# One state tile's matrix terms summed on GpSimd, and two output products moved on TensorE

## The chip, the cores and the metric

The kernel runs on one core of a Trainium2 chip. The metric is the device time of one launch in microseconds; lower is better. TensorE multiplies, VectorE, ScalarE and GpSimd (POOL in the profile) work on tiles, and SyncE (SP) issues the transfers. Each has its own queue and works through it in order; they meet through semaphores.

## What is computed

Two blocks of two layers on a sequence of 256 rows of width 1024, all in float32. The change lies in the last layer, whose mixer is this:

```python
def odd_mixer(h, w_in, ...):
    z = h @ w_in
    su, gc, ca, cb, gd = jnp.split(z, [...], axis=-1)
    y = s5_ssm(su, ...)
    ya, yb = jnp.split(y @ glu_w + glu_b, 2, axis=-1)
    ssm_out = ya * jax.nn.sigmoid(yb) * jax.nn.silu(gc)
    conv_out = conformer_conv(ca, cb, dw, ...) * jax.nn.silu(gd)
    return jnp.concatenate([ssm_out, conv_out], axis=-1) @ w_out
```

`s5_ssm` runs a complex linear recurrence over time, x(t) = a x(t-1) + (B u)(t), in 32 groups of 64 states, and reads it out as y = Re(C x) + d u = C_re x_re - C_im x_im + d u. `conformer_conv` is a gated causal convolution of 31 taps for each channel, a layer norm, a silu and one more product.

## The kernel before

**Weights.** A weight matrix comes in pieces of 512 rows by 512 columns (1 MB). SyncE loads a piece into a raw buffer, ScalarE rounds it to `w_hi` (L1600), VectorE subtracts to get the rest, `w_lo` (`split`, L1988), and TensorE forms each product from three: hi by hi, hi by lo, lo by hi. Both `w_hi` and `w_lo` are rings of three pieces. Three late pieces have their subtraction on GpSimd (`split`, L2851), the first half of the GLU weight among them. In the last mixer a group of 512 columns has two pieces, one for each half of the 1024 rows; `features_out` walks over the pieces i = 0, 1 and in each over four column blocks j = 0 to 3, and runs, after block (i, j), what its table `after` names. In a piece's first block the products that need `w_lo` come last (L919), after a wait for that piece's subtraction.

**The recurrence.** The 2048 states are in 16 tiles of 128, and four of these make one state tile j of the program (j = 0 to 3, 128x1024 elements for the real part and as many for the imaginary). The complex decay is turned into a real one: TensorE forms the drive (`drive(j)`, L1483), VectorE turns it by the angle -wt (`turn_back`, L2564 to L2570, which read PSUM) and scans along time with the real decay (`scan`, L2579), and GpSimd turns the result back by +wt: `turn_states(j)` forms four products with tables, x_re sin and x_im sin into `s5_o` (L2793), then x_re cos and x_im cos in place (L2796). With that

y = C_re (x_re cos) - C_re (x_im sin) - C_im (x_re sin) - C_im (x_im cos).

`outputs(j)` on TensorE (L1499) adds these four as products of 32 columns each, four column blocks apiece. The last two terms have the same matrix, and for the tiles in `SUMMED` (L112: tiles 2 and 3) they are added first, so TensorE has three products. Tile 2's sum is GpSimd's (L2801). Tile 3 has a function of its own, `turn_last_states`: GpSimd does two sine products (L2811, L2812) and one cosine product (L2814), VectorE the other (L2623) and the sum (L2631). VectorE then adds d u to the result (`outputs`, L2585) and splits y into `y_hi` and `uT_hi`.

Each tile's output comes into the same bank, `s5_o` is one buffer for all tiles, and `s5_x` is two, so `turn_states(j)` waits for `y_done` of the output before.

**The order around the change** is written out by hand. On GpSimd: tile 0, then `gate_conv` (L2784, the gate of the convolution's input), tile 1, the subtraction of a GLU piece, tile 2, tile 3, a root for the layer norm (L2688). On TensorE: column group GC with `drive(2)` after block (0, 0) and `outputs(0)` after block (0, 1); column group GD with `drive(3)` after the first piece and `outputs(1)` after block (1, 0); then the convolution as four blocks of eight tap groups (`convolve`, L1512), with `outputs(2)` ahead of block 2's last tap group; the GLU products; `outputs(3)` among them. On SyncE the 16 transfers that copy the gated input into `conv_stack` wait for `gate_conv`, and the GLU weight's two halves are loaded behind the first eight and behind all of them. On VectorE the subtractions of pieces stand between the steps of the recurrence: two after `scan(1)`, one after `turn_back(2)` (the second piece of GD) and one after `scan(3)`.

Of the kernel before, what the change touches and what calls it, by code (L numbers as in the profile page):

```python
# [44 lines left out]
HALF = 4  # L45
TAPS = 4
TAP_ROWS = 32
TAP_GROUPS = -(-CONV_K // TAPS)
# [60 lines left out]
RAW_ODD = (0, 1, 4, 0, 1, 4, 0, 1, 0, 2, 3, 1, 0)  # L109
RAW_SLOTS = [p % RAW_RING for p in range(RAW_SWITCH)] + list(RAW_ODD)  # L110
RAW_KEPT = 2
SUMMED = (2, 3)  # L112
WARM = 9
FIRST_PARTS = (((0, 1), (0,)), ((2, 3), (1, 2)), ((4, 5), (3, 4)), ((6, 7), (5, 6, 7)))
SPLIT_RING = 3
# [58 lines left out]
def build_program(nc, ins, consts, where, out):  # L174
    ctx = ExitStack()
    with ctx:
# [38 lines left out]
        def taps(a, group):  # L215
            if a < 5:
                return stack_a[:, a * channels + group, :]
            if a < 7:
                return stack_b[:, (a - 5) * channels + group, :]
            return stack_c[:, group, :]  # L220
# [650 lines left out]
        def _(pe):  # L871
# [90 lines left out]
            def features_out(n, p0, pieces, in_hi, in_lo, turn=None, after={}):  # L962


                assert turn is None
                for i in range(pieces):
                    p = p0 + i
                    pe.wait_ge(hi_ready, p + 1)
                    s = p % SPLIT_RING
                    for j in range(HALF):  # L970
                        if i == 0 and j % 2 == 0:
                            out_ready(n, j // 2)
                        at = slice(j * P, (j + 1) * P)
                        dst = OUT[j // 2][:, (j % 2) * SEQ:(j % 2 + 1) * SEQ]
                        parts = [(dst, w_hi[:, s, kk, at], w_lo[:, s, kk, at], in_hi[:, i * KP + kk, :],
                                  in_lo[:, i * KP + kk, :], True) for kk in range(KP)]
                        if j == 0:
                            last = products_upper(parts, p, i == 0, i == pieces - 1, shared=True)
                        else:
                            last = products(parts, i == 0 and j % 2 == 0, i == pieces - 1, shared=True)  # L980
                        if j == 1 and i == pieces - 1:
                            last.then_inc(out0_done, 1)
                        if j < HALF - 1 and (i, j) in after:
                            after[i, j]()
                    last.then_inc(piece_used, 1)
                    if (i, HALF - 1) in after:
                        after[i, HALF - 1]()
# [485 lines left out]
            def drive(j):  # L1473


                if j:
                    pe.wait_ge(drive_read, j)
                if j % 2 == 0:
                    pe.wait_ge(su_ready, j // 2 + 1)
                for b in range(2):  # L1480
                    for q in range(4):
                        rows_q = slice(32 * q, 32 * q + 32)
                        last = pe.matmul(bank[:, 4 + q, b * SEQ:(b + 1) * SEQ], b_mat[rows_q, b, j, :], su[rows_q, j, :],  # L1483
                                         start=True, stop=True)
                last.then_inc(drive_done, 1)

            def outputs(j):

                pe.wait_ge(states_ready, j + 1)
                if j == HALF - 1:  # L1490
                    pe.wait_ge(last_turned, 2)
                if j:
                    pe.wait_ge(y_lo, j)
                parts = [(0, s5_x[j % 2][0]), (1, s5_o[1]), (2, s5_x[j % 2][1])]
                if j not in SUMMED:
                    parts.insert(2, (2, s5_o[0]))
                for i, (m, states) in enumerate(parts):
                    for q in range(4):
                        last = pe.matmul(bank[32 * q:32 * q + 32, 2, 0:SEQ], c_mat[:, m, j, 32 * q:32 * q + 32], states[:, q, :],  # L1499
                                         start=(i == 0), stop=(i == len(parts) - 1))  # L1500
                last.then_inc(y_done, 1)

            def convolve(j, groups=range(TAP_GROUPS)):

                if j == 0 and groups[0] == 0:
                    pe.wait_ge(stack_landed, 16 * 4 * TAPS)
                    pe.wait_ge(taps_ready, 4)
                if j % 2 == 0 and groups[0] == 0:
                    pe.wait_ge(out_free[j // 2], O_USE + GD + 1)
                for a in groups:  # L1510
                    for q in range(4):
                        last = pe.matmul(OUT[j // 2][32 * q:32 * q + 32, (j % 2) * SEQ:(j % 2 + 1) * SEQ], taps(a, 4 * j + q),  # L1512
                                         conv_stack[:, j, q, TAPS * a:TAPS * a + SEQ], start=(a == 0), stop=(a == TAP_GROUPS - 1),
                                         skip_group_check=True)
                if j % 2:
                    last.then_inc(conv_done, 1)

            def block_out(p, blocks, banks, in_hi, in_lo, first, rows_ready):
# [12 lines left out]
                if blocks[-1] == KP - 1:  # L1531
# [3 lines left out]
                         after={(0, 0): turn_su, (0, 2): lambda: drive(0)})  # L1535
            features_out(O_USE + CB, O_PIECE + 2 * CB, 2, hT_hi, hT_lo,
                         after={(0, 0): lambda: drive(1)})
            features_out(O_USE + GC, O_PIECE + 2 * GC, 2, hT_hi, hT_lo,
                         after={(0, 0): lambda: drive(2), (0, 1): lambda: outputs(0)})
            features_out(O_USE + GD, O_PIECE + 2 * GD, 2, hT_hi, hT_lo,  # L1540
                         after={(0, HALF - 1): lambda: drive(3), (1, 0): lambda: outputs(1)})
            convolve(0)
            convolve(1)
            convolve(2, range(0, TAP_GROUPS - 1))
            outputs(2)
            convolve(2, range(TAP_GROUPS - 1, TAP_GROUPS))
            convolve(3)

            def y_rows(kk):
                pe.wait_ge(y_lo, kk + 1)  # L1550
# [1133 lines left out]
        def _(pool):  # L2684
# [101 lines left out]
            def turn_states(j):  # L2786
# [8 lines left out]
                for i, v in enumerate(s5_x[j % 2]):  # L2795
                    last = pool.tensor_tensor(v, v, cos, ALU.mult)  # L2796
                    if i == 0 or j in SUMMED:
                        order.mark(last)
                if j in SUMMED:
                    order.settle()  # L2800
# [125 lines left out]
```

## Time and profile before

| | |
|---|---|
| median of 3 runs | 992.45 us (992.42 to 992.67) |
| the profiled execution, its own time | 992.89 us |
| its span | 991.1 us |
| TensorE busy, share of the span | 984.2 us, 99% |
| VectorE busy | 732.6 us, 74% |
| ScalarE busy | 497.3 us, 50% |
| GpSimd busy | 129.8 us, 13% |

The profile is of one execution. Its span runs from the first instruction to the last, and the time of the execution is 1.8 us longer. A busy share is an average over the whole kernel: GpSimd's 13% lies mostly in the last 130 us, where it is the state tiles' engine and busy nearly without pause, and that is where the change is.

### The profile page before, as it was taken

The numbers are of one execution on the slowest core, as the hardware profiler recorded it, in microseconds if no ns is written. First come the engines' busy times: TensorE is split into PE (matmuls) and PEld (weight loads), VectorE is DVE, ScalarE is ACT, GpSimd is POOL, SyncE is SP. The second block draws the span as 40 slices with busy tenths as digits, with TensorE's granted clock in tenths as the row PEclk, the third lists the DMA queues.
The fourth block names the chain that finished last, engine by engine and source line by source line (L and its number), as shares of the span: only waits on it lengthen the run. The fifth ranks groups of instructions, "written<-read, shape, count | busy, mean of one in ns | idle before, by whom it ended". The sixth has DMA issues, their size and how long they took to land.

```text
span 991.1 us, 13299 instructions
## 1 busy us (share of the span) xinstructions
PE 984.2 (99%) x5502; PEld 835.6 (84%) x5502; DVE 732.6 (74%) x836; ACT 497.3 (50%) x596; POOL 129.8 (13%) x101
## 2 busy tenths in 40 slices
PE   9999999999999999999999999999999999999997
PEld 8888888888888888888888888888887899899796
DVE  5867786776656656677786777888877777789984
ACT  6545553554444345444563454444478554644252
POOL 0000000000000000000000030000000159169720
PEclk9999999999999999999999999999999999999999
DMA  9897796546655564697796667555554965345451
GB/s 362 300 280 266 234 281 209 197 168 212 197 185 170 185 216 132 192 300 247 234 273 219 222 176 243 200 184 207 170 173 153 300 193 173 126 170 155 112 191 43
DMA packets 116764, 204.33 MB, mean 206 GB/s; under 512 B 10209, under 2 KB 29665, under 8 KB 116449
## 3 DMA queue, kind: packets, MB, share of 16 engines
q1 hardware_dynamic: 116704, 203.50, 62.8%
q8 instruction: 43, 0.70, 0.3%
q14 instruction: 17, 0.13, 0.0%
HBM read 189.09 MB, written 12.06 MB: 203 GB/s over the span
## 4 chain that ended last, share of the span: by engine, by line
PE 99%; DVE 0%; ACT 0%; DVEq 0%; issue 0%; ACTq 0%
PE bank L887 13%; PE bank L889 13%; PE bank L890 13%; PE bank L1219 12%; PE bank L910 10%; PE bank L914 9%; PE bank L921 9%; PE bank L1223 6%; PE bank L1301 2%; PE bank L1512 1%; PE bank L1001 1%; PE bank L1091 1%; PE bank L919 1%; PE bank L912 1%; PE bank L1499 1%; PE bank L1173 1%
## 5 line engine op out<-in xcount | busy, mean ns | idle before, releaser
L1988 DVE TENSOR_TENSOR w_lo<-arena,w_hi 128x2048 fp32r<-128x2048 f32 (+1 forms) x79 | 181.5, 2309 | 80.5 <-ACT w_hi L1600 80.1
L1988 DVE TENSOR_TENSOR w_lo<-raw,w_hi 128x2048 fp32r<-128x2048 f32 (+1 forms) x78 | 178.1, 2293 | 70.3 <-ACT w_hi L1600 69.9
L1600 ACT ACTIVATE w_hi<-raw 128x2048 fp32r<-128x2048 f32 (+1 forms) x83 | 157.0, 1892 | 93.2 <-PE bank L890 63.8
L1600 ACT ACTIVATE w_hi<-arena 128x2048 fp32r<-128x2048 f32 (+1 forms) x79 | 149.4, 1891 | 97.7 <-PE bank L890 72.7
L1219 PE MATMUL bank<-hT,w_hi 128*128 128x512 f32 x504 | 123.4, 391 | 0.0
L1219 PEld LDWEIGHTS bank<-hT,w_hi 128*128 128x128 f32 x504 | 92.2, 188 | 17.6
L887 PE MATMUL bank<-w_hi,hT 128*128 128x512 f32 (+1 forms) x240 | 91.9, 383 | 0.0
L2688 POOL TENSOR_TENSOR rstd<-mean,const 128x1 f32<-128x1 f32 (+1 forms) x16 | 9.1, 578 | 628.0 <-DVE mean L1997 458.9
L889 PE MATMUL bank<-w_lo,hT 128*128 128x512 f32 (+1 forms) x224 | 85.5, 381 | 0.0
L890 PE MATMUL bank<-w_hi,hT 128*128 128x512 f32 (+1 forms) x224 | 85.5, 381 | 0.0
L887 PE MATMUL bank<-w_hi,uT_hi 128*128 128x512 f32 x208 | 81.1, 390 | 0.0
L890 PE MATMUL bank<-w_hi,uT_lo 128*128 128x512 f32 x208 | 80.9, 389 | 0.0
L889 PE MATMUL bank<-w_lo,uT_hi 128*128 128x512 f32 x208 | 80.9, 389 | 0.0
L910 PE MATMUL bank<-w_hi,hT 128*128 128x512 f32 (+1 forms) x208 | 79.8, 386 | 0.0
L914 PE MATMUL bank<-w_hi,hT 128*128 128x512 f32 (+1 forms) x208 | 78.9, 382 | 0.0
L1223 PEld LDWEIGHTS bank<-hT,w_lo 128*128 128x128 f32 x504 | 67.1, 191 | 3.9
L910 PE MATMUL bank<-w_hi,uT_hi 128*128 128x512 f32 x176 | 68.9, 392 | 0.0
L914 PE MATMUL bank<-w_hi,uT_lo 128*128 128x512 f32 x176 | 68.7, 390 | 0.0
L1223 PE MATMUL bank<-hT,w_lo 128*128 128x256 f32 x504 | 68.3, 282 | 0.0
L887 PE MATMUL bank<-hT,w_hi 128*128 128x256 f32 x192 | 55.3, 289 | 0.0
L921 PE MATMUL bank<-w_lo,hT 128*128 128x512 f32 (+1 forms) x208 | 53.9, 381 | 0.0
L887 PEld LDWEIGHTS bank<-w_hi,hT 128*128 128x128 f32 x240 | 45.1, 188 | 8.7
(339 smaller groups left out, 1854.4 us busy)
## 6 DMA issues: line engine op xcount, KB each, us to landing
arena<-in_w_in SPq DMA_DIRECT2D x21, 1024.0 KB, 5.3
raw<-in_w_in SPq DMA_DIRECT2D x20, 1024.0 KB, 7.0
arena<-in_w_up SPq DMA_DIRECT2D x16, 1024.0 KB, 5.7
raw<-in_w_up SPq DMA_DIRECT2D x16, 1024.0 KB, 5.8
arena<-in_w_down SPq DMA_DIRECT2D x16, 1024.0 KB, 5.1
raw<-in_w_down SPq DMA_DIRECT2D x16, 1024.0 KB, 5.1
raw<-in_e_w_in SPq DMA_DIRECT2D x6, 1024.0 KB, 5.5
arena<-in_e_w_in SPq DMA_DIRECT2D x6, 1024.0 KB, 5.3
```

Source lines behind the costliest of these rows:

```text
L887: pe.matmul(dst, a_hi, b_hi, start=first, stop=False, skip_group_check=shared)
L889: pe.matmul(dst, a_hi, b_lo, start=False, stop=False, skip_group_check=shared)
L890: mm = pe.matmul(dst, a_lo, b_hi, start=False, stop=last_one, skip_group_check=shared)
L910: pe.matmul(dst, a_hi, b_hi, start=(start and i == 0), stop=False, skip_group_check=shared)
L912: pe.matmul(dst, a_hi, b_lo, start=False, stop=False, skip_group_check=shared)
L914: pe.matmul(dst, a_lo, b_hi, start=False, stop=False, skip_group_check=shared)
L921: mm = pe.matmul(dst, a_hi, b_lo, start=False, stop=last_one, skip_group_check=shared)
L1219: pe.matmul(UP[j], w_hi[:, s[i], kk, at[j]], hT[:, k, :, :].rearrange("p e t -> p (e t)"), start=(i == kk == 0), stop=False, skip_group_ch ...
L1223: return pe.matmul(UP[j][:, 0:SEQ], w_lo[:, s[i], kk, at[j]], hT_hi[:, i * KP + kk, :], start=False, stop=(i == 1 and kk == KP - 1), skip_ ...
L1301: last = pe.matmul(OUT[t], a[:, KP * i + k, at[t]], w[:, s[i], k, :], start=(first and k == 0), stop=(last_one and k == KP - 1))
L1600: act.activation(w_hi[:, p % SPLIT_RING, :, 0:n], raw_at(p)[:, :, 0:n], copy).then_inc(hi_ready, 1)
L1988: dve.tensor_tensor(w_lo[:, s, :, 0:n], raw_at(p)[:, :, 0:n], w_hi[:, s, :, 0:n].bitcast(F32), ALU.subtract).then_inc(lo_ready, 1)
```

## The change

`SUMMED` gets tile 0. GpSimd then adds x_im cos and x_re sin of tile 0 after the four products, and `outputs(0)` has three products for four. `outputs(0)` moves from block (0, 1) of GC's first piece to behind its block (0, 3). `outputs(2)` moves behind the last tap group of convolution block 2 and the first two of block 3. The condition at `conv_done` keeps the count of that semaphore as it was, now that block 3 comes in two calls.

```diff
-SUMMED = (2, 3)
+SUMMED = (0, 2, 3)
...
-                if j % 2:
+                if j % 2 and groups[-1] == TAP_GROUPS - 1:
                     last.then_inc(conv_done, 1)
...
             features_out(O_USE + GC, O_PIECE + 2 * GC, 2, hT_hi, hT_lo,
-                         after={(0, 0): lambda: drive(2), (0, 1): lambda: outputs(0)})
+                         after={(0, 0): lambda: drive(2), (0, HALF - 1): lambda: outputs(0)})
...
             convolve(2, range(0, TAP_GROUPS - 1))
+            convolve(2, range(TAP_GROUPS - 1, TAP_GROUPS))
+            convolve(3, range(0, 2))
             outputs(2)
-            convolve(2, range(TAP_GROUPS - 1, TAP_GROUPS))
-            convolve(3)
+            convolve(3, range(2, TAP_GROUPS))
```

GpSimd's queue from tile 0 to tile 1, before: two sine products, two cosine products, `gate_conv`, and the first instructions of tile 1.

```order
L2793 TENSOR_TENSOR h_sb<-arena 128x1024 [waits scans_done]
L2793 TENSOR_TENSOR h_sb<-arena 128x1024
L2796 TENSOR_TENSOR arena<-arena 128x1024 [waits pool_order]
L2796 TENSOR_TENSOR arena<-arena 128x1024
L2784 TENSOR_TENSOR arena<-arena 128x4x256 [waits out_free1,out_free0]
L2793 TENSOR_TENSOR h_sb<-arena 128x1024 [waits y_done,scans_done]
```

The same place after the change (every line number here is one higher):

```order
L2794 TENSOR_TENSOR h_sb<-arena 128x1024 [waits scans_done]
L2794 TENSOR_TENSOR h_sb<-arena 128x1024
L2797 TENSOR_TENSOR arena<-arena 128x1024 [waits pool_order]
L2797 TENSOR_TENSOR arena<-arena 128x1024
L2802 TENSOR_TENSOR arena<-arena,h_sb 128x1024 [waits pool_order]
L2785 TENSOR_TENSOR arena<-arena 128x4x256 [waits out_free1,out_free0]
L2794 TENSOR_TENSOR h_sb<-arena 128x1024 [waits y_done,scans_done]
```

The add is new and waits for the products (`pool_order`); `gate_conv` and all of tile 1 stand one instruction later.

TensorE's queue at the third output, in the convolution (`const`, `stack_b` and `stack_c` hold the taps of groups 0 to 4, 5 and 6, and 7, four matmuls a group; L1499 is `outputs(2)`):

```order
 L1512 MATMUL bank<-arena,stack_b 32x256 x8
+L1512 MATMUL bank<-arena,stack_c 32x256 x4
+L1512 MATMUL bank<-arena,const 32x256 x8
 L1499 MATMUL bank<-arena,c_mat 32x256 [waits y_lo,states_ready]
 L1499 MATMUL bank<-arena,c_mat 32x256 x3
 L1499 MATMUL bank<-h_sb,c_mat 32x256 x4
 L1499 MATMUL bank<-arena,c_mat 32x256 x4
-L1512 MATMUL bank<-arena,stack_c 32x256 x4
-L1512 MATMUL bank<-arena,const 32x256 x20
+L1512 MATMUL bank<-arena,const 32x256 x12
```

Twelve matmuls (three tap groups) now stand ahead of the third output that stood behind it. In the trace each of these matmuls is two records.

## Rows read from the trace of the kernel before

**Rows 1.** The chain of waits over the whole span, shares by engine
```profile
PE 99%; DVE 0%; ACT 0%; DVEq 0%; issue 0%; ACTq 0%
```

**Rows 2.** Timeline of TensorE, first output (start us, us, engine, line, instructions)
```profile
901.72 0.64 PE L1499 MATMUL bank<-arena,c_mat 128*32 128x256 f32 x8
902.17 1.05 PE L1499 MATMUL bank<-h_sb,c_mat 128*32 128x256 f32 x16
903.03 0.61 PE L1499 MATMUL bank<-arena,c_mat 128*32 128x256 f32 x8
903.58 0.39 PE L887 MATMUL bank<-hT,w_hi 128*128 128x256 f32 x1
...
906.56 0.28 PE L910 MATMUL bank<-hT,w_hi 128*128 128x256 f32 x1
```

**Rows 3.** Timeline of TensorE around the second output
```profile
920.30 0.64 PE L919 MATMUL bank<-hT,w_lo 128*128 128x256 f32 x4
...
920.87 0.64 PE L1499 MATMUL bank<-arena,c_mat 128*32 128x256 f32 x8
```

**Rows 4.** Timeline of TensorE, first rows of the third and last outputs
```profile
937.20 0.61 PE L1499 MATMUL bank<-arena,c_mat 128*32 128x256 f32 x8
...
949.30 0.64 PE L1499 MATMUL bank<-arena,c_mat 128*32 128x256 f32 x8
```

**Rows 5.** Timeline of GpSimd, 896 to 948 us (x2: two instructions)
```profile
896.39 4.76 POOL L2796 TENSOR_TENSOR arena<-arena 128x1024 f32<-128x1024 f32 x2
...
901.09 2.21 POOL L2784 TENSOR_TENSOR arena<-arena 128x1024 f32<-128x1024 f32 x1
...
912.40 4.78 POOL L2796 TENSOR_TENSOR arena<-arena 128x1024 f32<-128x1024 f32 x2
...
919.82 4.60 POOL L2851 TENSOR_TENSOR w_lo<-raw,w_hi 128x2048 fp32r<-128x2048 f32 x1 [2.64 <-DVE w_lo L1988]
...
924.82 4.77 POOL L2793 TENSOR_TENSOR h_sb<-arena 128x1024 f32<-128x1024 f32 x2 [0.40 <-DVE arena L2579]
...
934.49 2.39 POOL L2801 TENSOR_TENSOR arena<-arena,h_sb 128x1024 f32<-128x1024 f32 x1
...
938.85 2.79 POOL L2811 TENSOR_TENSOR h_sb<-arena 128x1024 f32<-128x1024 f32 x1 [1.98 <-PE bank L1499]
...
941.60 2.39 POOL L2812 TENSOR_TENSOR h_sb<-arena 128x1024 f32<-128x1024 f32 x1
...
944.07 3.26 POOL L2814 TENSOR_TENSOR arena<-arena 128x1024 f32<-128x1024 f32 x1
```

**Rows 6.** Timeline of GpSimd, the two sine products of tile 1, each by itself
```profile
903.83 4.07 POOL L2793 TENSOR_TENSOR h_sb<-arena 128x1024 f32<-128x1024 f32 x1 [0.53 <-PE bank L1499]
907.86 4.46 POOL L2793 TENSOR_TENSOR h_sb<-arena 128x1024 f32<-128x1024 f32 x1
```

**Rows 7.** Timeline of VectorE, two weight splits in a row, each by itself
```profile
903.37 2.26 DVE L1988 TENSOR_TENSOR w_lo<-raw,w_hi 128x2048 fp32r<-128x2048 f32 x1
905.55 4.49 DVE L1988 TENSOR_TENSOR w_lo<-raw,w_hi 128x2048 fp32r<-128x2048 f32 x1
```

**Rows 8.** Timeline of VectorE, single rows from 898 to 949 us
```profile
898.70 4.75 DVE L2579 TENSOR_TENSOR_SCAN arena<-bank,arena 128x256 f32<-128x256 f32 x8
...
917.45 2.29 DVE L1988 TENSOR_TENSOR w_lo<-arena,w_hi 128x2048 fp32r<-128x2048 f32 x1
...
937.13 2.27 DVE L1988 TENSOR_TENSOR w_lo<-raw,w_hi 128x2048 fp32r<-128x2048 f32 x1
...
941.68 3.39 DVE L2623 TENSOR_TENSOR arena<-arena 128x1024 f32<-128x1024 f32 x1 [1.01 <-POOL h_sb L2811]
...
947.27 1.21 DVE L2631 TENSOR_TENSOR arena<-arena,h_sb 128x1024 f32<-128x1024 f32 x1
```

**Rows 9.** Timeline of ScalarE, split of the first half of the GLU weight
```profile
915.96 1.92 ACT L1600 ACTIVATE w_hi<-raw 128x2048 fp32r<-128x2048 f32 x1 [2.56 <-DMA raw<-in_o_glu_w]
```

**Rows 10.** Timeline of SyncE's queue, load of that half
```profile
908.68 1.26 SPq L703 DMA_DIRECT2D raw<-in_o_glu_w  x1
```

## The prediction, written before the changed kernel ran

> **What bounds the kernel now.** I read the chain of waits first: it is TensorE for 99% of the span [rows 1]. So time is won only by giving TensorE less to do, and lost wherever it has to wait. The timeline of TensorE, from 901 us to the end, shows no idle row: at each of the four output products the gap ahead is about 0.1 us beyond the usual spacing, after weights of another shape, and not a wait. Then I read the timelines of the engines that feed it, to see how close to TensorE's need each of them delivers.
>
> Two deliveries are close. The lower half of the second weight piece of group GD, a VectorE subtraction at 917.45, ends at 917.45 + 2.29 = 919.74 [rows 8]; TensorE starts the four products that read it at 920.30 [rows 3]. And VectorE's sum for the last output ends at 947.27 + 1.21 = 948.48 [rows 8]; that output starts at 949.30 [rows 4]. The slack is 0.56 and 0.82 us.
>
> The third thing to see is that GpSimd and VectorE do not run side by side when VectorE reads both inputs from SBUF. GpSimd's sine product of a 128x1024 tile takes 2.39 us alone [rows 5], but 4.07 and 4.46 us while VectorE splits weights [rows 6]; in that stretch the second of two splits takes 4.49 us where the first took 2.26 [rows 7]. The starts interleave: split 1 until 905.6, product 1 until 907.9, split 2 until 910.0, product 2 until 912.3. Each waits for the other's instruction to end, and the one that waits goes next. Scans and operations on PSUM do not do this: two cosine products took 4.76 us beside VectorE's scan [rows 5, 8]. The Trainium skill ("SBUF — State Buffer", Who interferes with whom) says just this: a VectorE instruction with two SBUF inputs and a GpSimd one that reads SBUF exclude each other for the whole instruction, and issue order decides who is blocked. It is the rule that speaks against this change, and the trace agrees.
>
> **The change, part by part.**
>
> *One product fewer.* In the first output 16 matmul records on h_sb take 903.03 - 902.17 = 0.86 us [rows 2], so the eight of one term take 0.43. TensorE gains **0.43 us**.
>
> *The first output stands later.* It moves behind the other half of the group's first piece, which ran from 903.58 to 906.56 [rows 2], some 2.9 us without the switch of weights; so it starts at 901.7 + 2.9, about 904.6. It needs GpSimd's new add. The cosine products end at 896.39 + 4.76 = 901.15; with the 0.08 us that such a settle costs and 2.39 us for an add [rows 5] the states are ready at **903.6**. No wait: 1 us of slack. The move itself costs nothing.
>
> *The add on GpSimd.* 2.39 us, beside a scan on VectorE, so the price is not there but behind it. In the queue behind it stand gate_conv (2.21 us, before at 901.09 [rows 5]) and the four products of the second tile. I replay the exclusion with the measured times:
> - split 1 is issued at 903.37 and waits for the add, which lets go at about 903.5; the next VectorE instruction starts at 905.7.
> - gate_conv, which ran free before, now waits for split 1: it ends at 907.9. Split 2 then: VectorE is free at 909.95, as before, when split 2 ended at 905.55 + 4.49 = 910.04 [rows 7].
> - VectorE's chain is thus unmoved: its third split is issued at about 917.45 again.
> - GpSimd's first sine product ends at 912.3, where before the *second* ended. The four products end 2.3 us later than the 917.18 of before (912.40 + 4.78 [rows 5]), at 919.5, and the last cosine product starts at 917.1, **0.3 us ahead of the split**. So the split waits until 919.4 and ends at 919.4 + 2.26 = **921.7**.
>
> TensorE reaches the products that read it at 920.30 - 0.43 = 919.87. A wait's release, a weight load and the first matmul take another 0.1, so they start at about 921.8: TensorE stands **1.5 us later** than before (921.8 - 920.3), the saving already in it. The wait is 1.9 us. The second output needs states at 920.87 before; they are ready at 919.5, so it waits for nothing more.
>
> *SyncE, ScalarE.* gate_conv releases the 16 transfers of the convolution stack and, between them, half a GLU weight. gate_conv ends 4.6 us later, so that load's issue moves from 908.68 [rows 10] to 913.3 and ScalarE's split of it from 915.96 [rows 9] to 920.5; it ends at 922.45. GpSimd's own split of that piece (919.82 before [rows 5]) starts then, 2.6 us later, and the third tile's first product at 927.1, not 924.82. The third states were ready at 934.49 + 2.39 = 936.88; now about 939.2.
>
> *The third output stands later.* Three column groups of the convolution pass ahead of it; the one that it already skips and two more, 8 records each, at 0.43: 1.3 us. TensorE comes to it at 937.20 + 1.5 + 1.3 = 940.0 [rows 4]. That is past 939.2, so the move covers GpSimd's delay; at its old place TensorE would have waited some 0.5 us. But the last tile's GpSimd work waits for this output's end. It started at 938.85 [rows 5], now 938.85 + 2.8 = 941.65. Before, it was held for 0.4 us (2.79 against 2.39) by the split at 937.13 [rows 8]; that split, 1.9 late too, is over at 941.3. First sine 944.05, second 946.4 (before 941.60 + 2.39 = 943.99), so 2.4 later. VectorE's cosine product, which before ran 3.39 us for the same exclusion [rows 8], the third GpSimd product and VectorE's sum keep their distances: the sum ends at 948.48 + 2.4 = 950.9. TensorE gets to the last output at 949.30 + 1.5 = 950.8 and starts at about 951.0. That is another 0.15.
>
> *After that* only the rows of TensorE count; ScalarE and VectorE follow it with the same shift.
>
> **Sum.** -0.43 + 1.93 (wait for the split) + 0.15 (last output) = **+1.65 us**. The profiled execution took 992.89, 0.44 over the median of 992.45; against the median that is **994.1**. If nothing were blocked, the sum would be -0.43 and the result 992.0; 0.43 is also all the change can win.
>
> Bounds of the unknown: the order at 903.5 and at 917, and how fast the GLU load lands once it starts later, between the 7.3 us of before (908.68 to 915.96) and about 8.5.
>
> **The rivals.**
> 1. *GpSimd goes first at 903.5* (gate_conv ahead of split 1). For: its instruction is already in its queue when the add ends. Against: at 905.6 and 907.9 the engine that waited went next. Then both splits run later, VectorE is 2.35 us late at 912.3, its third split is no longer blocked but ends at 922.05; TensorE stands 1.9 later there, 2.05 at the end: 994.5.
> 2. *The third split gets in ahead of the last cosine product* (margin 0.3 us). Then TensorE has its weights, but the states of the second tile come at 922.0 against 920.87 - 0.43: 1.2 later, and 1.45 after the last output: 993.9.
> 3. *The load lands late.* Each us past 0.8 us of slack on the third states goes to TensorE, and to the last tile's chain behind it: 994.6 to 995.2.
> 4. *Not slower.* GpSimd's queue has room after all: if the add and gate_conv pass while VectorE scans and its splits do not meet them, cosine products end by 919.4 with the split done in time (it has 0.13 us of slack left against 919.87). It decides at one blocked instruction less, 2.2 us, between 903 and 917. Price -0.43 to +0.1: 992.0 to 992.6. Against: between 901.15 and 919.87 stand one add, gate_conv, four products and three splits, 2.39 + 2.2 + 9.6 + 6.6 = 20.8 us, in 18.7 us, and they exclude each other.
>
> **How the numbers follow.** Forecast 0.57; rival 1, 0.12; rival 2, 0.10; rival 3, 0.12; rival 4, 0.07; 0.02 for anything else. Forecast and rivals 1 and 2 share a cause and lie at 993.9 to 994.5; each carries some 0.5 us for what I read off the starts of rows. The range 993.3 to 995.0 leaves out rival 4 and the far end of rival 3, some 0.13. What a measurement can tell from no change is about 0.2%, 1.98 us, so the border is 994.43, just above my forecast. Faster by that much is out of reach of 0.43: 0.01. Within it lie most of the forecast's own spread (0.6 us), rivals 2 and 4: 0.63. Slower: rivals 1 and 3 and a part of the forecast, 0.36.
>
> **What would show it.** In the new profile: an idle row of TensorE, about 1.9 us, ahead of the L919 products near 921.8, released by VectorE's split; that split 4.2 us long; gate_conv longer than 4 us, ending near 907.9; GpSimd's second-tile products ending near 919.5; the first transfer of the stack near 908; a short wait at the last output. I am wrong if L919 starts before 920.5, or if the first or third output has a wait ahead of it.

## The result, and the profile after

The changed kernel takes 994.45 us in the median of 13 executions, the kernel before 992.45 in as many; the ratio is 1.0021 with a 95% interval of 1.0013 to 1.0029. Measured a second time, 11 executions: 994.19 us, 1.0019 (1.0010 to 1.0028). So the change makes the kernel slower by 1.6 to 2.0 us (the second time the kernel before, run beside it, had a median of 992.56). That is small, but both intervals lie above 1: it is a loss and not noise. One of the first 13 executions took 1999.65 us, with 128x512 matmuls of 674 ns where they take 391 otherwise, and it is the one that was profiled; so what follows is the profile of an execution of the second measurement, 994.33 us long with a span of 992.5.

| | before | after |
|---|---|---|
| median | 992.45 us | 994.45 us, again 994.19 |
| profiled execution, its span | 992.89, 991.1 us | 994.33, 992.5 us |
| executions of the first measurement, lowest to highest (without the one of 1999.65) | 992.35 to 992.79 | 993.86 to 996.02 |

The last row is news: the changed kernel is spread over 2.2 us. The kernel before stays within 0.5 us here, and within 1.0 us (992.23 to 993.26) in all its 104 executions beside the kernels below.

TensorE's waits in the last 190 us, for which the kernel before has no row at all (columns: engine, tile, line, released by: us in total, times, longest):

```profile
PE bank L919 <- DVE w_lo L1989: 1.6, 1, 1.6
```

TensorE's timeline of the same kernel, at its four outputs and the products of the late weight piece:

```profile
904.44 0.64 PE L1499 MATMUL bank<-arena,c_mat 128*32 128x256 f32 x8
904.89 0.61 PE L1499 MATMUL bank<-h_sb,c_mat 128*32 128x256 f32 x8
905.32 0.61 PE L1499 MATMUL bank<-arena,c_mat 128*32 128x256 f32 x8
905.87 0.39 PE L910 MATMUL bank<-hT,w_hi 128*128 128x256 f32 x1
...
921.47 0.74 PE L919 MATMUL bank<-hT,w_lo 128*128 128x256 f32 x4 [1.60 <-DVE w_lo L1989]
...
922.14 0.64 PE L1499 MATMUL bank<-arena,c_mat 128*32 128x256 f32 x8
...
939.74 0.61 PE L1499 MATMUL bank<-arena,c_mat 128*32 128x256 f32 x8
...
950.72 0.64 PE L1499 MATMUL bank<-arena,c_mat 128*32 128x256 f32 x8
```

The first output now takes 905.87 - 904.44 = 1.43 us where it took 903.58 - 901.72 = 1.86 [rows 2]: the 0.43 us are won. Then TensorE stands idle ahead of L919, which starts at 921.47 and not at 920.30 [rows 3]. From there to the last output it takes 950.72 - 921.47 = 29.25 us, 0.25 more than before [rows 3, 4]. Together the last output starts 950.72 - 949.30 = 1.42 us later, and that is the whole difference of the two profiled executions (994.33 - 992.89 = 1.44 us).

GpSimd's timeline of the changed kernel (x2: two instructions in one row):

```profile
901.06 2.40 POOL L2802 TENSOR_TENSOR arena<-arena,h_sb 128x1024 f32<-128x1024 f32 x1
903.42 4.25 POOL L2785 TENSOR_TENSOR arena<-arena 128x1024 f32<-128x1024 f32 x1
907.63 6.83 POOL L2794 TENSOR_TENSOR h_sb<-arena 128x1024 f32<-128x1024 f32 x2
914.53 4.74 POOL L2797 TENSOR_TENSOR arena<-arena 128x1024 f32<-128x1024 f32 x2
922.13 4.59 POOL L2852 TENSOR_TENSOR w_lo<-raw,w_hi 128x2048 fp32r<-128x2048 f32 x1 [2.87 <-ACT w_hi L1601]
926.68 4.77 POOL L2794 TENSOR_TENSOR h_sb<-arena 128x1024 f32<-128x1024 f32 x2
...
936.37 2.38 POOL L2802 TENSOR_TENSOR arena<-arena,h_sb 128x1024 f32<-128x1024 f32 x1
941.40 2.39 POOL L2812 TENSOR_TENSOR h_sb<-arena 128x1024 f32<-128x1024 f32 x1 [2.65 <-PE bank L1499]
```

VectorE's timeline, the splits and the sum for the last output:

```profile
903.22 6.60 DVE L1989 TENSOR_TENSOR w_lo<-raw,w_hi 128x2048 fp32r<-128x2048 f32 x2
...
917.22 4.19 DVE L1989 TENSOR_TENSOR w_lo<-arena,w_hi 128x2048 fp32r<-128x2048 f32 x1
...
938.81 2.27 DVE L1989 TENSOR_TENSOR w_lo<-raw,w_hi 128x2048 fp32r<-128x2048 f32 x1
...
949.41 1.21 DVE L2632 TENSOR_TENSOR arena<-arena,h_sb 128x1024 f32<-128x1024 f32 x1
```

Read the three together. The add takes 2.40 us beside a scan. `gate_conv`, 2.21 us before [rows 5], takes 4.25, because the first split is in its way. The pair of splits takes 6.60, as before. The two cosine products run from 914.53 to 919.27, and the third split, issued at 917.22 while the second of them runs, takes 4.19 us for 2.29 [rows 8]. It ends at 921.41, and TensorE goes on 0.06 later.

One thing said of GpSimd ahead of the prediction was too strong. It is not busy nearly without pause over the last 130 us: there it is busy 69.3 of 131 us. Around the change it nearly is, 50.0 of the 57 us from 893 to 950.

### The profile page after: what moved, and what is told of

It is laid out like the page before. It is cut to its first block, busy times and chain, and to the rows that moved or that the text cites. A ratio compares the mean times of both kernels' runs of the same rounds, so it can differ in the third digit from the quotient of the medians.

```text
span 1997.8 us, 13284 instructions
## 1 busy us (share of the span) xinstructions
PE 1991.1 (100%) x5494; PEld 1392.2 (70%) x5494; DVE 738.8 (37%) x836; ACT 502.0 (25%) x596; POOL 117.2 (6%) x102
## 4 chain that ended last, share of the span: by engine, by line
PE 100%; DVE 0%; ACT 0%; DVEq 0%; issue 0%; ACTq 0%
PE bank L887 13%; PE bank L890 13%; PE bank L889 13%; PE bank L1219 12%; PE bank L910 10%; PE bank L921 9%; PE bank L914 9%; PE bank L1223 6%; PE bank L1301 2%; PE bank L1512 1%; PE bank L1001 1%; PE bank L1091 1%; PE bank L912 1%; PE bank L919 1%; PE bank L1499 1%; PE bank L1173 1%
## 5 line engine op out<-in xcount | busy, mean ns | idle before, releaser
L1219 PE MATMUL bank<-hT,w_hi 128*128 128x512 f32 x504 | 245.8, 674 | 0.0
L1219 PEld LDWEIGHTS bank<-hT,w_hi 128*128 128x128 f32 x504 | 149.0, 304 | 70.3 <-issue 63.3
L887 PE MATMUL bank<-w_hi,hT 128*128 128x512 f32 (+1 forms) x240 | 159.0, 663 | 0.0
L889 PE MATMUL bank<-w_lo,hT 128*128 128x512 f32 (+1 forms) x224 | 147.5, 659 | 0.0
L890 PE MATMUL bank<-w_hi,hT 128*128 128x512 f32 (+1 forms) x224 | 145.7, 650 | 0.0
L887 PE MATMUL bank<-w_hi,uT_hi 128*128 128x512 f32 x208 | 140.8, 677 | 0.0
L889 PE MATMUL bank<-w_lo,uT_hi 128*128 128x512 f32 x208 | 139.7, 671 | 0.0
L890 PE MATMUL bank<-w_hi,uT_lo 128*128 128x512 f32 x208 | 139.6, 671 | 0.0
L1223 PEld LDWEIGHTS bank<-hT,w_lo 128*128 128x128 f32 x504 | 125.8, 324 | 17.8 <-issue 16.6
L910 PE MATMUL bank<-w_hi,hT 128*128 128x512 f32 (+1 forms) x208 | 138.0, 664 | 0.0
L914 PE MATMUL bank<-w_hi,hT 128*128 128x512 f32 (+1 forms) x208 | 136.9, 659 | 0.0
L1223 PE MATMUL bank<-hT,w_lo 128*128 128x256 f32 x504 | 128.2, 440 | 0.0
L914 PE MATMUL bank<-w_hi,uT_lo 128*128 128x512 f32 x176 | 119.1, 677 | 0.0
L910 PE MATMUL bank<-w_hi,uT_hi 128*128 128x512 f32 x176 | 119.0, 676 | 0.0
L921 PE MATMUL bank<-w_lo,hT 128*128 128x512 f32 (+1 forms) x208 | 104.6, 655 | 0.0
L889 PEld LDWEIGHTS bank<-w_lo,hT 128*128 128x128 f32 x224 | 70.2, 314 | 34.3 <-issue 31.6
L921 PE MATMUL bank<-w_lo,uT_hi 128*128 128x512 f32 x176 | 91.3, 674 | 0.0
```

The source lines that it names most:

```text
L887: pe.matmul(dst, a_hi, b_hi, start=first, stop=False, skip_group_check=shared)
L889: pe.matmul(dst, a_hi, b_lo, start=False, stop=False, skip_group_check=shared)
L890: mm = pe.matmul(dst, a_lo, b_hi, start=False, stop=last_one, skip_group_check=shared)
L910: pe.matmul(dst, a_hi, b_hi, start=(start and i == 0), stop=False, skip_group_check=shared)
L914: pe.matmul(dst, a_lo, b_hi, start=False, stop=False, skip_group_check=shared)
L921: mm = pe.matmul(dst, a_hi, b_lo, start=False, stop=last_one, skip_group_check=shared)
```

## The experiments

Apart from the repetition, each kernel takes one or two causes away or puts one in another place. `small_add`, `small_gate`, `small_cosine` and `cosine_load` leave out a part of the arithmetic and `four_products` counts a term twice: their times tell what a piece of work costs, and none of them is a kernel to use. Each was timed beside the kernel before, whose medians in three groups were 992.56 (the first four), 992.43 (the next four) and 992.48 (the last four). "Exclusion theory" in the expectations is the prediction's account: GpSimd and VectorE hold each other up, and VectorE's third split comes late.

### The changed kernel again

> The changed kernel once more, for a profile of an execution at full TensorE clock. Exclusion theory: 994.1 to 994.5; the third split on VectorE (L1989, near 917.4) lasts about 4.2 us because the last cosine product of tile 1 holds it up, gate_conv (L2785) lasts over 4 us, and TensorE waits about 1.9 us ahead of the L919 products near 921.8. Rival, the moved outputs: no wait there, but waits at the third or the last output that sum to 2 us.

994.19 us. The rows above are its profile: the wait, the long split and the long `gate_conv` are there.

### The moves without the sum

```diff
-SUMMED = (0, 2, 3)
+SUMMED = (2, 3)
```

> SUMMED is (2, 3) again, both outputs stay where the change puts them. Exclusion theory: the moves alone cost the 1.3 us by which the third output's end is late, less 0.8 us of slack at the last output and 0.4 us that GpSimd's first product of tile 3 no longer waits: 992.5 to 992.9. If the moves are the cause, nearly the whole loss stays: 994.3 or more.

992.69 us (992.42 to 992.99), ratio 1.0000 (0.9992 to 1.0009). The moves cost next to nothing, as foreseen. They are cleared, and the loss needs the sum. VectorE's third split is already held here, 4.26 us long, and does no harm: it ends at 918.97, and TensorE is there at 919.76. Its row on VectorE:

```profile
914.71 4.26 DVE L1989 TENSOR_TENSOR w_lo<-arena,w_hi 128x2048 fp32r<-128x2048 f32 x1
```

### The sum on a sixteenth of the time steps

```diff
-                    last = pool.tensor_tensor(s5_x[j % 2][1], s5_x[j % 2][1], s5_o[0], ALU.add)
+                    part = slice(0, 16 if j == 0 else SEQ)
+                    last = pool.tensor_tensor(s5_x[j % 2][1][:, :, part], s5_x[j % 2][1][:, :, part], s5_o[0][:, :, part], ALU.add)
```

> The change with GpSimd's add of tile 0 on 16 of 256 time steps (the other steps of that sum are left out, so that matrix term is incomplete); TensorE still has three products. Exclusion theory: the add's 2.2 us are what pushes the rest of GpSimd's queue back; without them gate_conv and tile 1 stand where they stood, the third split lasts 2.3 us, and the 0.43 us of the product is a gain: 992.0 to 992.4. If the moves are the cause: 994 or more.

992.38 us (992.19 to 992.66). TensorE has all of the change's relief and order here, and the loss is gone: without the add's 2 us on GpSimd there is none. But not all of the story in the expectation is right. GpSimd's and VectorE's timelines of this kernel (first GpSimd):

```profile
901.13 2.20 POOL L2785 TENSOR_TENSOR arena<-arena 128x1024 f32<-128x1024 f32 x1
905.90 6.44 POOL L2794 TENSOR_TENSOR h_sb<-arena 128x1024 f32<-128x1024 f32 x2 [2.57 <-PE bank L1499]
912.42 4.77 POOL L2797 TENSOR_TENSOR arena<-arena 128x1024 f32<-128x1024 f32 x2
```

```profile
903.00 4.69 DVE L1989 TENSOR_TENSOR w_lo<-raw,w_hi 128x2048 fp32r<-128x2048 f32 x2
...
915.09 4.25 DVE L1989 TENSOR_TENSOR w_lo<-arena,w_hi 128x2048 fp32r<-128x2048 f32 x1
```

The third split is held here as well, 4.25 us. GpSimd stands idle until 905.90 for the first output's end, so the two splits of the pair run nearly undisturbed, 4.69 us for 6.60, and VectorE comes to its third split 2.1 us sooner, again behind a cosine product that has begun. I had expected the split to be short. What decides is not whether it is held but when the product ahead of it ends: here at 917.19, in the changed kernel at 919.27, and each time the split ends 2.1 us behind it, at 919.34 and 921.41. TensorE wants its result at 919.49 here.

### The gate on a sixteenth of the time steps

```diff
-                pool.tensor_tensor(c_at, c_at, gate_d[:, :, :], ALU.mult).then_inc(conv_gated, 1)
+                pool.tensor_tensor(c_at[:, :, 0:16], c_at[:, :, 0:16], gate_d[:, :, 0:16], ALU.mult).then_inc(conv_gated, 1)
```

> The change in full, but gate_conv multiplies 16 of 256 time steps (the gate of the convolution's input is left out on the rest). Exclusion theory: GpSimd has 2 us less to do between the add and the second tile, so the last cosine product ends near 917.7 and the third split near 919.9, when TensorE needs it: 992.1 to 992.8. If the add's own delay of the first output were the cause, this would change nothing: 994.3.

992.27 us (992.04 to 992.76). The add is whole here, and the loss is gone again. It is not the add as such: 2 us less at another place in GpSimd's queue do the same. The last cosine product ends at 917.46 and the third split, held for 4.22 us, at 919.61, in time for TensorE at 919.74. Two things go together in this kernel, since `gate_conv` also ends 1.8 us sooner than in the changed one and releases its transfers sooner.

### Four products again, beside the sum

```diff
-                if j not in SUMMED:
+                if j not in SUMMED or j == 0:
```

> The change, but TensorE forms the first output of four products again (the sine term is then counted twice in tile 0; nothing else differs). Exclusion theory: TensorE stands idle until VectorE's third split anyway, so the 0.43 us of the product only shortens that wait: 994.0 to 994.4, the same as the change, and the wait ahead of L919 is 1.2 us for 1.6. If the saved product is a gain that the rest merely outweighs: 994.6.

994.64 us in the median (993.89 to 996.18): outside the range that I gave, and the rival's figure. But the executions are spread over 2.3 us, and the lowest are 993.89 and 993.92, where the changed kernel's lowest are 993.86 and 994.01: the product made no difference to the shortest executions. The profile is of its slowest execution. TensorE's timeline there:

```profile
921.79 0.74 PE L919 MATMUL bank<-hT,w_lo 128*128 128x256 f32 x4 [1.22 <-DVE w_lo L1989]
...
941.30 0.64 PE L1499 MATMUL bank<-arena,c_mat 128*32 128x256 f32 x8 [1.04 <-POOL arena L2802]
```

The wait at L919 is 1.22 us, 0.38 shorter, as the exclusion theory has it: the saved product only lengthens a wait. And there is a second wait, at the third output. ScalarE's timeline of this execution, and then of the changed kernel, shows where it starts:

```profile
922.58 1.91 ACT L1601 ACTIVATE w_hi<-raw 128x2048 fp32r<-128x2048 f32 x1 [9.08 <-DMA raw<-in_o_glu_w]
```

```profile
920.08 1.91 ACT L1601 ACTIVATE w_hi<-raw 128x2048 fp32r<-128x2048 f32 x1 [7.28 <-DMA raw<-in_o_glu_w]
```

The half GLU weight, whose load now stands behind a later `gate_conv`, landed 2.5 us later in the one than in the other. GpSimd's split of it, its tile 2 and with them the third states came later by as much. A later issue is not needed for that: in `small_add` the same load is issued at 908.69, as in the kernel before (908.68 [rows 10]), and ScalarE gets it at 919.04 and not at 915.96 [rows 9].

### The last cosine product of tile 1 on a sixteenth

```diff
-                    last = pool.tensor_tensor(v, v, cos, ALU.mult)
+                    part = slice(0, 16 if i == 1 and j == 1 else SEQ)
+                    last = pool.tensor_tensor(v[:, :, part], v[:, :, part], cos[:, :, part], ALU.mult)
```

> The change, but GpSimd's last cosine product of tile 1 covers 16 of 256 time steps (the turn of that part is left out on the rest). Add and gate_conv stay. Exclusion theory: the third split is no longer held, lasts 2.3 us and ends near 919.6, TensorE does not wait ahead of L919: 992.1 to 992.7. If the later gate_conv with its transfers is the cause (it ends at 907.7 here too): 994.

993.62 us (993.29 to 994.31): between the two figures, and a miss. The split does last 2.29 us, and no wait is left ahead of L919. TensorE's timeline shows what is left:

```profile
919.75 0.64 PE L919 MATMUL bank<-hT,w_lo 128*128 128x256 f32 x4
...
939.42 0.64 PE L1499 MATMUL bank<-arena,c_mat 128*32 128x256 f32 x8 [1.30 <-POOL arena L2803]
```

I had counted only one of the two things that the late GpSimd queue moves. The other, `gate_conv` and the load behind it, ends in a wait of 1.3 us at the third output (this profile is of the slowest execution, 994.31 us, so in the median one the wait is probably shorter). In the changed kernel that wait is hidden by the first one: its third states are ready at 938.75, and TensorE comes at 939.74 only because it stood idle ahead of L919. They are two causes side by side, and the later one counts.

### The second half's load earlier

```diff
                 if s == 1:
                     load(square_piece(ins["o_glu_w_2"][0], 0, 0))
-            load(square_piece(ins["o_glu_w_2"][0], 1, 0))
+                if s == 2:
+                    load(square_piece(ins["o_glu_w_2"][0], 1, 0))
```

> The change, with the load of the GLU weight's second half put ahead of the last four stack transfers. In the profile of the changed kernel ScalarE waited for that load until 929.7, between two steps that free TensorE's banks and split y. Exclusion theory: the median stays, 994.0 to 994.3, since the wait ahead of L919 does not depend on it; the load explains the executions above 994.6 if it explains anything, and they should be gone. If late transfers are the main cause: 993.0 or less.

995.82 us in 5 executions (995.37 to 996.17): worse than the change, and a second miss. TensorE's waits in this kernel's last 190 us:

```profile
PE bank L1513 <- DMA arena<-arena: 1.8, 1, 1.8
PE bank L920 <- DVE w_lo L1990: 1.6, 1, 1.6
```

The megabyte went ahead of the last four stack transfers (of the sixteen into `conv_stack`), and the convolution (L1513) waited 1.8 us for them. So the stack, whose first transfer is issued 4.4 us later than before, is a third thing that the late `gate_conv` brings near the edge: its last transfer lands 5.9 us ahead of the convolution in the kernel before (921.33 and 927.24), 2.6 us ahead in the changed kernel and 0.5 us ahead in `small_cosine`.

### GpSimd waits for the split

```diff
+                    if i == 1 and j == 1:
+                        piece_split(pool, O_PIECE + 2 * GD + 1)
                     last = pool.tensor_tensor(v, v, cos, ALU.mult)
...
-                         after={(0, HALF - 1): lambda: drive(3), (1, 0): lambda: outputs(1)})
+                         after={(0, HALF - 1): lambda: drive(3), (1, 1): lambda: outputs(1)})
```

> The change, with GpSimd's last cosine product of tile 1 made to wait for VectorE's third split, and the second output one block later on TensorE, where its states are ready. Exclusion theory: the split lasts 2.3 us and TensorE does not wait ahead of L919, but the cosine product ends 2.2 us later and the third and last outputs wait in turn, 1.1 and 0.2 us: 993.2 to 993.8. If the split's hold is not the cause: 994.2 or more.

993.76 us (993.21 to 994.46). The split is 2.29 us again, L919 does not wait, and the rest has moved to the second, third and last output (0.27, 0.95 and 0.37 us in its profile).

### The first half's load ahead of everything

```diff
+            load(square_piece(ins["o_glu_w_2"][0], 0, 0))
             sp.wait_ge(conv_gated, 1)
             piece_split(sp, RAW_SWITCH - 1)
...
-                if s == 1:
-                    load(square_piece(ins["o_glu_w_2"][0], 0, 0))
```

This edit was laid on the change, on `small_cosine` and on `split_first`.

> The change, with the load of the GLU weight's first half ahead of the stack transfers and of their wait for gate_conv. Two-cause theory (the held split sets the floor, the load, late behind gate_conv, sets the spread above it): the floor stays, the spread goes: median 993.8 to 994.2, highest 994.5 or less. If the spread has nothing to do with this load, it stays up to 996.

994.28 us (993.99 to 996.25). The floor (the shortest executions) stays. The spread stays too: 4 of 10 executions took 995.68 or more, though this load, with ScalarE at 912.35 in the profile, can hardly be late. That part of the expectation is wrong.

> small_cosine together with load_first (the last cosine product of tile 1 on 16 of 256 steps). small_cosine alone kept 1.2 us of the loss, by the profile as a wait of the third output for states that come after the GLU load. Two-cause theory: without the late load that wait is gone too: 992.1 to 992.6, the figure of small_add. If something else behind gate_conv is the cause: 993.3 or more.

992.26 us (991.94 to 992.93). With both causes taken away the whole loss is gone. It is 0.2 us below the kernel before, where the product would give 0.43; the interval (0.9988 to 1.0006) doesn't tell that from nothing. TensorE has no wait in the last 190 us of its profile.

> split_first together with load_first; nothing is left out. GpSimd's split of the GLU piece then starts behind the last cosine product at 921.7 and not at 922.4, so third and last output wait less: 992.9 to 993.4, between the change and the kernel before. If the load is no cause: 993.8.

993.19 us (993.00 to 993.65). Nothing is left out here; with this order and this load the change costs 0.7 us, ratio 1.0007 (0.9998 to 1.0015), and repeats well. About 1 us of the loss is recovered, but it is no better than the kernel before. GpSimd's timeline:

```profile
914.30 2.41 POOL L2798 TENSOR_TENSOR arena<-arena 128x1024 f32<-128x1024 f32 x1
919.35 2.40 POOL L2798 TENSOR_TENSOR arena<-arena 128x1024 f32<-128x1024 f32 x1 [2.63 <-DVE w_lo L1988]
921.71 4.61 POOL L2853 TENSOR_TENSOR w_lo<-raw,w_hi 128x2048 fp32r<-128x2048 f32 x1
```

### The sum without the moves

> The kernel before with SUMMED (0, 2, 3) alone; both outputs stay at their old places. The first output, reached at 901.7, must wait for states that come at 903.5: 1.9 us. By the exclusion theory that is lost once, not twice, since TensorE would have waited for the third split anyway: 993.8 to 994.5. If the two waits add: 996 or more.

994.62 us (994.17 to 995.54), a little above the range, and far from 996. TensorE's timeline:

```profile
903.17 0.64 PE L1499 MATMUL bank<-arena,c_mat 128*32 128x256 f32 x8 [1.86 <-POOL arena L2801]
...
921.32 0.64 PE L919 MATMUL bank<-hT,w_lo 128*128 128x256 f32 x4
...
939.29 0.64 PE L1499 MATMUL bank<-arena,c_mat 128*32 128x256 f32 x8 [0.90 <-POOL arena L2801]
```

The first output waits 1.86 us, and then L919 does not wait at all. It starts at about the time of the changed kernel (921.32 for 921.47), but by TensorE's own lateness: the held split ended at 921.11, 0.2 us before. So the delay is paid once, as expected, at one place or the other. The third output, at its old place, waits 0.90 us, and in the changed kernel it does not wait. That its move saves this much is argued: no kernel has the sum and only that output at its old place, and the two moves together are worth 0.2 to 0.4 us in the medians (994.62 against 994.45 and 994.19), less than the spread of either kernel.

## Why the prediction was right, and where it was not

**Time.** 994.1 was forecast; 994.45 and 994.19 were measured, inside 993.3 to 995.0. As a ratio the first is 0.21% and the second 0.19%, on both sides of the border that I drew at 0.2%, so the 0.63 that I gave to the one side and the 0.36 to the other are neither borne out nor refuted. The sum can be compared term by term in the two profiles: -0.43 + 1.93 + 0.15 = 1.65 us were forecast. TensorE could have gone on at 919.72 (920.30 - 0.43, and 0.15 us sooner in this execution) and did at 921.47, which is 1.75 for 1.93 (the 1.60 us of the wait's row are counted from the end of the matmul before, and the release and the next start come on top); with 0.25 for 0.15 the sum is 1.57, less the 0.15 of the earlier start 1.42. The shortest executions differ by about as much (993.86 and 992.35 us). That the medians of the first measurement differ by more, 2.0 us, goes with the long executions, which the forecast of 994.1 does not contain: 4 of 23 took more than 995.0, and nothing in the sum stands for them.

**The product, 0.43 us.** Right as a relief of TensorE (1.43 us for 1.86), and as that a gain only where TensorE then has no wait. In the change it is none; in the kernels in which TensorE waits for no data (`small_add`, `small_gate`, `cosine_load`) 0.2 to 0.3 us are left in the medians, and no interval tells that from nothing.

**The first output moved, no cost.** Right: 904.44 without a wait, forecast 904.6, and the stage begins 0.15 us earlier in this execution (VectorE's first split at 903.22 for 903.37).

**The replay of the exclusion.** Right row by row: `gate_conv` to 907.67 (forecast 907.9), cosine products to 919.27 (919.5), the third split 4.19 us to 921.41 (921.7), L919 at 921.47 (921.8). Less the 0.15 us, each is within 0.2. The order at 903.5 (rival 1) and the 0.3 us by which the last cosine product got ahead of the split (rival 2) came out as I took them. The rule of the Trainium skill ("SBUF — State Buffer", Who interferes with whom) holds here in every row that I looked at: an instruction that finds the other engine at work takes its own 2.2 to 2.4 us plus what was left of the other's.

**The late load.** Half right. The load's issue moved to 913.59 (forecast 913.3), ScalarE's split to 920.08 (920.5), GpSimd's to 922.13 (922.45), the third states to 938.75 (939.2), ahead of TensorE at 939.74 (940.0). But I carried the landing as a side rival of 0.12, with "each us past 0.8 us of slack", and took 7.3 to about 8.5 us from issue to landing. The rows have 6.5 us in the changed kernel, 9.2 in the profiled execution of `four_products` and 10.3 in `small_add`, outside it on both sides. In the execution of `four_products` with 996.18 us the late load did what the rival says. What I failed to see is that it is a second cause and not only a risk: with the first one gone it alone keeps 1.2 us (`small_cosine`), against 1.8 us with the first one alone (`load_first`), which is why my expectation for `small_cosine` missed.

**The last output.** Forecast +0.15 us; 0.25 us appear between L919 and the last output: about 0.10 at the L919 products, which take 0.67 us to the next start for 0.57, and 0.17 ahead of the last output, which stands 0.38 us behind the matmul before it for 0.21, since VectorE's sum ends at 950.62.

**Not slower (rival 4)** fell, by its own sum: 20.8 us of work that excludes itself in 18.7 us. `small_add` and `small_gate` take away about 2 of them each, and the loss goes.

**Open.** Why some executions take 995.6 to 996.3. The late load explains most of the one of `four_products` that was profiled, but `load_first`, where it can hardly be late, still has four such in ten, and none of these four was profiled. Executions of 995.4 us or more appear in every kernel in which TensorE loses over 1 us ahead of L919 or of the first output (the change, `four_products`, `early_load`, `load_first`, `sum_only`), and in none of the seven others, whose longest took 994.46. The stack transfers are a candidate, since late ones cost TensorE 1.8 us in `early_load`; but there the edit put a load ahead of them, and there is no profile of a long execution of the change or of `load_first` to tell.

## What to carry to other kernels

When two engines exclude each other, count their work together: add up everything that both must do between two deadlines, and a spare engine at 13% busy may turn out to have no room just there. Follow every release of an instruction that is pushed back, the transfers too; here one added instruction pushed back a weight split, a weight load and sixteen copies at once, and removing one cause only uncovered the next. Work taken off the engine that bounds the kernel is a gain only if that engine's next data are there sooner too.

## What the runs showed of the hardware

- GpSimd's products and VectorE's splits, which read both inputs from SBUF, exclude each other instruction by instruction, and in these rows the waiting one goes next. A 128x1024 product of 2.21 us on GpSimd takes 4.25 beside a split; a 128x2048 split of 2.29 us on VectorE takes 4.19 beside a product. A small instruction waits as long as a large one: GpSimd's `gate_conv` on 16 steps (`small_gate`) takes 2.35 us behind a split, where its add on 16 steps takes 0.32 us beside a scan (`small_add`). If the two engines only shared a rate, the small one would be done soon. The two rows on GpSimd:

```profile
903.48 2.35 POOL L2785 TENSOR_TENSOR arena<-arena 128x64 f32<-128x64 f32 x1
```

```profile
900.86 0.32 POOL L2803 TENSOR_TENSOR arena<-arena,h_sb 128x64 f32<-128x64 f32 x1
```

- The landing of one and the same 1 MB load, issued at 913.33 and 913.59, differed by 2.5 us between two executions (ScalarE began on it at 922.58 and 920.08). Issued at 908.69 it came at 919.04 in `small_add`, issued at 908.68 at 915.96 in the kernel before.
- An idle time of 1.6 us did not lower TensorE's granted clock in the profile: it reads 1.00 in the 5 us before, around and after the wait.
